# One core, a two-layer decoder trunk: one ring of three PSUM banks in the attention stage, the attention's rows first in the output product, and the convolution's norm moved to the last attention rounds

## The reference, cut to what matters

```python
def conv_sparse_attn_mixer(h, pos, n_keys, w_in, conv_w, conv_b, ln_g, ln_b, w_out):
    a_val, a_gate, q, k, v, qi, ki, wi = jnp.split(h @ w_in, offsets, axis=-1)
    a = a_val * jax.nn.sigmoid(a_gate)
    a = jax.nn.silu(layer_norm(causal_depthwise_conv(a, conv_w, conv_b), ln_g, ln_b))   # 512 channels, width 31
    ...
    o = sparse_index_attention(q, k, v, qi, ki, wi, topk).reshape(bsz, length, ATT_WIDTH)  # 8 heads of 64
    return jnp.concatenate([a, o], axis=-1) @ w_out                                     # (1024, 1024)
```

## Time and profile before

| | us |
|---|---|
| median of 3 runs (lowest, highest) | 2590.16 (2589.67, 2592.37) |
| the profiled execution's own time | 2592.61 |
| its span, first to last instruction | 2590.8 |
| attention stage, first scores to last `normalise` | 391.0 to 623.8 |
| output product of layer 0: first matmul, start of its third block | 630.86, 657.45 |
| PE busy, span | 2412.0 (93%) |
| DVE busy, span | 2029.2 (78%) |
| ACT busy, span | 1684.9 (65%) |

### The profile page before, as it was taken

The page is one execution under the profiler, slowest core; times in us unless marked ns, Lnnn a source line. Parts: engine busy times, 40 slices in busy tenths (PEclk is TensorE's granted clock), DMA queues, the critical chain, the costliest instruction groups (busy, mean ns, idle before and its releaser), DMA issues. The chain is left out here.

```text
span 2590.8 us, 37548 instructions
## 1 busy us (share of the span) xinstructions
PE 2412.0 (93%) x12649; PEld 2071.5 (80%) x12649; DVE 2029.2 (78%) x2588; ACT 1684.9 (65%) x1815; POOL 643.5 (25%) x481
## 2 busy tenths in 40 slices
PE   8989998986979999999999599998979999999997
PEld 8969978874867888888888499996867888888885
DVE  3788876776888999899988543547778998998886
ACT  3369836666227887888887465663147878887775
POOL 0105814353012222222221412121002222222223
PEclk9999999997988999999999699999979999999998
DMA  5502354324339699988898411114259699999994
GB/s 173 141 6 93 82 98 132 100 67 127 108 140 379 228 354 370 363 330 325 310 375 295 179 57 33 41 33 154 96 202 346 237 348 371 374 373 367 376 371 181
DMA packets 121517, 565.80 MB, mean 218 GB/s; under 512 B 23735, under 2 KB 32183, under 8 KB 72144
## 3 DMA queue, kind: packets, MB, share of 16 engines
q1 hardware_dynamic: 96304, 513.25, 54.8%
q0 software_dynamic: 25120, 51.36, 7.2%
HBM read 575.32 MB, written 73.28 MB: 250 GB/s over the span
## 5 line engine op out<-in xcount | busy, mean ns | idle before, releaser
L2197 DVE TENSOR_TENSOR e0wlo<-e0raw,e0whi 128x2048 fp32r<-128x2048 f32 x214 | 487.1, 2290 | 59.9 <-ACT e0whi L2045 59.9
L2045 ACT ACTIVATE e0whi<-e0raw 128x2048 fp32r<-128x2048 f32 x214 | 409.8, 1915 | 92.3 <-PE e0banks L94 78.3
L2197 DVE TENSOR_TENSOR e1wlo<-e1raw,e1whi 128x2048 fp32r<-128x2048 f32 x138 | 313.1, 2286 | 42.4 <-ACT e1whi L2045 42.4
L2045 ACT ACTIVATE e1whi<-e1raw 128x2048 fp32r<-128x2048 f32 x138 | 263.9, 1913 | 42.5 <-PE e1banks L94 36.4
L92 PE MATMUL e0banks<-e0whi,e0xh 128*128 128x512 f32 x576 | 231.1, 401 | 1.1 <-DVE e0xl L2202 1.1
L94 PE MATMUL e0banks<-e0whi,e0xl 128*128 128x512 f32 x576 | 226.4, 393 | 0.0
L93 PE MATMUL e0banks<-e0wlo,e0xh 128*128 128x512 f32 x576 | 225.9, 392 | 0.0
L2197 DVE TENSOR_TENSOR e_wu<-e1raw,e_wu 128x2048 fp32r<-128x2048 f32 x70 | 160.3, 2292 | 17.3 <-ACT e_wu L2045 17.3
L92 PE MATMUL odd_banks<-h2T_hi,odd_w_hi 128*128 128x348 f32 x480 | 171.5, 357 | 0.8 <-DVE h2T_lo L2517 0.5
L2045 ACT ACTIVATE e_wu<-e1raw 128x2048 fp32r<-128x2048 f32 x70 | 134.2, 1918 | 49.0 <-PE e1banks L94 30.1
L93 PE MATMUL odd_banks<-h2T_lo,odd_w_hi 128*128 128x348 f32 x480 | 155.1, 323 | 0.0
(11 more groups left out here) (516 smaller groups left out, 6875.2 us busy)
## 6 DMA issues: line engine op xcount, KB each, us to landing
e0raw<-in_moe_w_gate SPq DMA_DIRECT2D x72, 1024.0 KB
e0raw<-in_moe_w_up SPq DMA_DIRECT2D x72, 1024.0 KB
e0raw<-in_moe_w_down SPq DMA_DIRECT2D x72, 1024.0 KB
e1raw<-in_moe_w_gate SPq DMA_DIRECT2D x70, 1024.0 KB
e1raw<-in_moe_w_up SPq DMA_DIRECT2D x70, 1024.0 KB
e1raw<-in_moe_w_down SPq DMA_DIRECT2D x70, 1024.0 KB
qki_w_raw<-in_w_even SPq DMA_DIRECT2D x22, 512.0 KB, 5.8
pre<-in_conv_band SPq DMA_DIRECT2D x32, 320.0 KB, 3.0
```

The costliest lines, as they stand in the source:

```text
L2045: act.activation(w_hi[i], raw[:, i, :], ACT.Copy).then_inc(hi_done[i], 1)
L2197: dve.tensor_tensor(w_lo[i], raw[:, i, :], w_hi[i].bitcast(F32), ALU.subtract).then_inc(lo_done[i], 1)
```

## The change

- **Banks.** `c_ps` is gone; `t_ps` has three banks, and everything small goes through them as a ring in one fixed order of uses (`ring_order`): transposed groups, convolution groups, denominators, means, variances. Each use waits until the use three places ahead of it has been read (`bank_free`). The scores of blocks 0 to 3 go to the third bank of `s_ps`, those of blocks 4 to 7 to the first two, block 8 to all three; PE waits only for the last step that shares a bank.
- **Convolution.** Groups run in the rounds n with n % 7 not 1, 3 or 5 (four of seven), the last in round 49. ACT takes a group before the late part of `p_high`.
- **Norm.** The means are one burst of 8 groups per tile, in rounds 9, 23, 37 and 51, summed by DVE. POOL, not DVE, centres, behind all its head splits; POOL's split of the output weights comes after that. ACT squares in rounds 57 to 60, variances in 58 to 61, each added by DVE; root in 63, scaling in 65 to 68, tanh in 67 to 70, last product in 69 to 72.
- **Rows through DRAM.** The eight stores stay in the attention's block, but nothing in it waits for them; the wait and the four loads are the first thing that SP does in the output product.
- **Output product of layer 0.** The attention's rows (and their weights) come first. PE makes rows 0 to 3 of block 0, rows 0 to 3 of block 1, then rows 4 to 7 of block 0, then rows 4 to 7 of block 1. ACT and DVE split the inputs of the first two pieces, then weight rows 2 to 7, then the inputs of the last two. Layer 1 keeps its order.

```diff
-GROUP_ROUNDS = [n for n in range(N) if n % 3 != 2][:CG - FIRST_GROUPS]
+GROUP_ROUNDS = [n for n in range(N) if n % 7 not in (1, 3, 5)][:CG - FIRST_GROUPS]
...
-MEAN_AT, CENTRE_AT, VAR_AT, ROOT_AT, SCALE_AT, SWISH_AT, OUT_AT = (CONV_STEPS + n for n in (1, 6, 8, 13, 15, 17, 18))
+MEAN_IN = {GROUP_ROUNDS[W4 * (t + 1) - 1 - FIRST_GROUPS] + 2: t for t in range(CT)}
+CENTRE_AT, VAR_AT, ROOT_AT, SCALE_AT, SWISH_AT, OUT_AT = (CONV_STEPS + n for n in (6, 8, 13, 15, 17, 19))
+T_RING = 3
...
+def ring_order():
+
+    uses = [("conv", g) for g in range(FIRST_GROUPS)]
+    at, norm_at, k = [None] * N, [], 0
+    for n in range(-1, ROUNDS):
+        conv = [("conv", GROUP_IN[n])] if n in GROUP_IN else []
+        turned = []
+        if n + 1 < N:
+            at[n + 1] = k
+            turned = [("turned", k + i) for i in range(len(key_groups(STEPS[n + 1][1])))]
+            k += len(turned)
+        uses += turned[:EARLY_GROUPS] + conv + turned[EARLY_GROUPS:] if late_conv(n) else conv + turned
...
+        def score_banks(b):
+            first, last = (2, 3) if WIDTH[b] <= 512 else (0, -(-WIDTH[b] // 512))
+            return range(first, last)
...
-            sp.wait_ge(stored, 16 * PH)
-            for t in range(CT):
-                sp.dma_start(aT[:, t, :], a_d[P * t:P * (t + 1), :, :].rearrange("c r n -> c (r n)")).then_inc(a_loaded, 16)
             sp.wait_ge(loaded, 64 * HEADS)
-            sp.wait_ge(a_loaded, 16 * CT)
...
             for h in range(1, HEADS):
-                if h == HEADS - 1:
-                    ahead.split_all(pool, out_hi, out_lo)
                 for part in range(4):
                     split(h, part)
+            pool.wait_ge(mean_done, CT)
+            for t in range(CT):
+                pool.tensor_tensor(tile(t), tile(t), every(mean), ALU.subtract).then_inc(cen_done, 1)
+            ahead.split_all(pool, out_hi, out_lo)
...
+            def bank_free(*use):
+                i = nth_use[use] - T_RING
+                kind, k = uses[i] if i >= 0 else ("none", 0)
+                if kind == "turned":
+                    pe.wait_ge(t_free, k + 1)
+                elif kind == "conv":
+                    pe.wait_ge(conv_done, k + 1)
+                elif kind == "mean":
+                    pe.wait_ge(mean_done, k + 1)
+                elif kind == "var":
+                    pe.wait_ge(var_done, k + 1)
+                else:
+                    pe.wait_ge(ready, 1)
...
-                if n:
-                    pe.wait_ge(s_read, n)
+                before = [m for m in range(n) if set(score_banks(STEPS[m][1])) & set(score_banks(b))]
+                if before:
+                    pe.wait_ge(s_read, before[-1] + 1)
...
+    PLAN = [(what, i) for k in range(ahead.split - 1, K)
+            for what, i in [("weights", k)][k < ahead.split:] + [("piece", i) for i, one in enumerate(pieces) if one[3] == k]]
...
         def _(sp):
+            if load_more is not None:
+                load_more(sp)
             for k in range(A, K):
...
-            product(0)
-            pe.wait_ge(p_loaded, 64)
+            for n, k0, k1, _ in pieces[:-1]:
+                run(n, [(k, j) for k in range(k0, k1) for j in range(2)])
+            _, k0, k1, _ = pieces[-1]
+            last_run = [(k, j) for j in range(2) for k in range(k0, k1)]
...
+            def load_conv(sp):
+                sp.wait_ge(conv_stored, 16 * PH)
+                for t in range(CT):
+                    sp.dma_start(aT[:, t, :], a_d[P * t:P * (t + 1), :, :].rearrange("c r n -> c (r n)")).then_inc(a_loaded, 16)
...
-            mix_out(nc, "m0", const, [(aT, CT, True), (oT, 4, False)], A["w_out0"],
-                    A["h0"], A["ln_mix0"], A["wr0"], A["rb0"], h1_d, s1_d, logits, picks, 0, ahead, (4, 4), score[:, 0:4 * D])
+            mix_out(nc, "m0", const, [(oT, 4, False), (aT, CT, True)], A["w_out0"],
+                    A["h0"], A["ln_mix0"], A["wr0"], A["rb0"], h1_d, s1_d, logits, picks, 0, ahead,
+                    [(0, 0, 4, 1), (1, 0, 4, 1), (0, 4, 8, 7), (1, 4, 8, 7)], score[:, 0:4 * D], load_conv, {2: conv_loaded})
```

More of the change, by code:

```diff
@@ L962 @@
 AHEAD, EARLY_GROUPS, DEN_AFTER = 3, 2, 2
[L965 to L977, removed]
+ROUNDS = N + 3 * DEN_AFTER
 def denominator_at(n):
@@ L1223, in _ @@
             turned(0, False)
-            for n in range(N + 3 * DEN_AFTER):
-                three = n + 1 < N and len(key_groups(STEPS[n + 1][1])) > EARLY_GROUPS
+            for n in range(ROUNDS):
                 if n + AHEAD < N:
                     scores(n + AHEAD)
-                if n in GROUP_IN and not three:
+                if n in GROUP_IN and not late_conv(n):
                     taps(GROUP_IN[n])
@@ L1231, in _ @@
                     turned(n + 1, True)
-                if n in GROUP_IN and three:
+                if n in GROUP_IN and late_conv(n):
                     taps(GROUP_IN[n])
@@ L1239, in _ @@
                     denominators(t, g)
-                if MEAN_AT <= n < MEAN_AT + MEAN_STEPS:
-                    means(range((n - MEAN_AT) * CG // MEAN_STEPS, (n + 1 - MEAN_AT) * CG // MEAN_STEPS))
+                if n in MEAN_IN:
+                    means(MEAN_IN[n])
                 if VAR_AT <= n < VAR_AT + CT:
@@ L1638, in split @@
                 ins.then_inc(x_hi_done, 1)
-            split_first(0)
-            for k in range(S, K):
-                act.wait_ge(loaded[k % RAW], 16 * (k // RAW + 1))
-                act.activation(w_hi[k], raw[k % RAW], ACT.Copy).then_inc(w_hi_done, 1)
-                if k - S + 1 < len(first_parts):
-                    split_first(k - S + 1)
-            split(1)
+            for what, k in PLAN:
+                if what == "piece":
+                    split_piece(k)
+                else:
+                    act.wait_ge(loaded[k % RAW], 16 * (k // RAW + 1))
+                    act.activation(w_hi[k], raw[k % RAW], ACT.Copy).then_inc(w_hi_done, 1)
             for n, b in enumerate(blocks):
@@ L1683, in add_bias @@
                 dve.wait_ge(l_done, n + 1)
-            split_first(0)
-            for k in range(S, K):
-                dve.wait_ge(w_hi_done, k - S + 1)
-                dve.tensor_tensor(w_lo[k], raw[k % RAW], w_hi[k].bitcast(F32), ALU.subtract).then_inc(w_lo_done, 1)
-                if k - S + 1 < len(first_parts):
-                    split_first(k - S + 1)
+            for what, k in PLAN:
+                if what == "piece":
+                    split_piece(k)
+                else:
+                    dve.wait_ge(w_hi_done, k - S + 1)
+                    dve.tensor_tensor(w_lo[k], raw[k % RAW], w_hi[k].bitcast(F32), ALU.subtract).then_inc(w_lo_done, 1)
             link(dve.tensor_copy(picks.tri[:].rearrange("p a n -> p (a n)"), const[:, C_TRI:C_TRI + 2 * P]))
-            split(1)
             dve.wait_ge(p_loaded, 64)
@@ L1728, in _, with run @@
         def _(pe):
-            def product(n, beside=None):
+            def run(n, order, beside=None):
                 q = toks(blocks[n])
-                if n:
-                    pe.wait_ge(x_lo_done, n)
-                if n >= 2:
-                    pe.wait_ge(normed, 2 * n - 2)
-                order = [(k, j) for k in range(K) for j in range(2)] if n == 0 else [(k, j) for j in range(2) for k in range(K)]
                 for i, (k, j) in enumerate(order):
-                    if n == 0 and k >= S:
+                    if n < 2 and j == 0:
+                        pe.wait_ge(first_lo, 1 + next(i for i, one in enumerate(pieces) if one[0] == n and one[1] <= k < one[2]))
+                    if n < 2 and k >= S:
                         pe.wait_ge(w_lo_done, k - S + 1)
-                    if n == 0 and j == 0 and k in starts:
-                        pe.wait_ge(first_lo, starts.index(k) + 1)
                     last = mm3(pe, y_ps2[n % 2][0:q, j, :], (x_hi[:, n % 2, k, 0:q], x_lo[:, n % 2, k, 0:q]),
@@ L1746, in product @@
                         beside(i)
+            def product(n, beside=None):
+                pe.wait_ge(x_lo_done, n - 1)
+                pe.wait_ge(normed, 2 * n - 2)
+                run(n, [(k, j) for j in range(2) for k in range(K)], beside)
             def turn(n):
@@ L1785, in beside @@
                             turn(n)
-                product(n + 1, beside)
+                if n == 0:
+                    run(1, last_run, beside)
+                    pe.wait_ge(p_loaded, 64)
+                else:
+                    product(n + 1, beside)
                 if last:
```

168 lines of the change are left out of this document (97 added, 71 removed).

## The result

The changed kernel takes 2610.47 us (median of 4 runs, 2606.71 to 2613.55) against 2591.26 of the one before (4 runs). The medians are 19.2 apart; the ratio is 1.0068 (17.6), 95% interval 1.0056 to 1.0080, so 14.5 to 20.7 slower. The prediction said 2594 and a range to 2603: the time lies outside the range, and slower had 0.43 against 0.42 for no change, which is no call of the side. The profiled execution took 2613.55 (span 2611.8), the longest of the four. Times are microseconds.

What follows compares the result with a forecast made beforehand. PE bounds attention up to round 44, then waits for DVE, table loads and ACT. Attention's gain of 21.0 is outweighed by a late norm and open trip: 660.8 - 657.45 + 0.5 = +3.9, so 2594 against the median; range 2585 to 2603.

Steps and rivals of the forecast that it cites:

- the third block: Output product's third block on PE: forecast to start at 660.8 against 657.45 before.
- the clock: TensorE's clock around the output product's two pauses: +0.5 taken, up to 3 as the bound.
- rounds 0 to 44: Attention's first part: third bank removes most PE waits for low parts; gain 5, between ends of 0 and 8.
- the trip: Stores, loads and weights from the norm's end to the third block's start: little hidden now, +44.8.
- Rounds 45 to 66: Attention's later rounds: 84.1 becomes 68.1, gain 16.0, from DVE's centring and the tanh leaving; ends 10 and 22.
- POOL's centring: Four centrings on POOL against rounds 57 to 60: 9.7 in all, just fits, priced at nothing; bound +4.
- The rival: Rounds 57 to 60: head 7's load or slow POOL centring holds ACT; +4 to +9, 2598 to 2603; chance 0.20.
- The tail: Last rounds, limited by ACT: norm ends 25.7 after step 68's high part, at 616.0; attention near 618.
- The rival without new waits: Last rounds: tanh of tiles 2 and 3 finds its slot free, norm ends 4 to 5 earlier; 2589.5; chance 0.15.
- In the rest PE is the limit and the start is passed on: After the third block's start: its delay of 660.8 against 657.45 carries through to the end unchanged.
- the first rival: Attention up to round 66: PE never starved, gain 8 + 22.7, not 21.0; 2584.5; chance 0.14.
- the parts named for "slower": Verdict slower than 2595.3: rest of the forecast, POOL and the cold clock; given 0.43.

Runs made afterwards that it cites:

- entry_banks: Changed kernel with the first two convolution groups in the output banks, off the ring; ratio to the kernel before 1.0053, 3.9 faster than the changed kernel.
- own_bank: Changed kernel without the shared ring: two banks for transposes and denominators, the third for convolution, means and variances, first three groups not waiting for a memset; ratio 1.0074.
- norm_early: Changed kernel with convolution groups in two of three rounds again, POOL's centrings ahead of its split of head 7; ratio to the kernel before 1.0009.
- weights_first: Changed kernel with SP issuing the weights' rows 4 to 7 ahead of the loads of the convolution's rows; ratio to the kernel before 1.0049.
- product_next_round: Changed kernel with the norm's last product one round behind the tanh, not two; ratio to the kernel before 1.0049, 4.9 faster than the changed kernel.
- mended: Changed kernel with the diffs of entry_banks, product_next_round and tile_stores; ratio to the kernel before 0.9999, 18 faster than the changed kernel.
- tile_stores: Changed kernel with the convolution's rows stored tile by tile behind each product, 32 quarter stores for 8; ratio to the kernel before 1.0027.
- early_mended: Changed kernel with the diffs of norm_early, entry_banks, product_next_round and tile_stores, and the old output product; median 2578.15 us, ratio to the kernel before 0.9943.
- before_tile_stores: Kernel before the change with its stores issued tile by tile behind each product of the norm; ratio to the kernel before 0.9979, 5.4 faster.

## Why the prediction was wrong

It put the third block 3.4 behind (3.9 with the clock); it is 15.45 behind. The step that failed most is the first of the sum, rounds 0 to 44, which was to win 5 and lost 2.9. The entry (3.1) and the backlog behind the third block (2.5) were put at nothing, and the trip was 4.0 short. The mechanism that made it slower, a norm that ends late with its trip open behind it, was forecast. Step by step, with the norm's end 8.1 later than forecast and the way from there 4.0 longer:

- **The stage before**, untouched, ended 2.1 later in this execution. No forecast could have it, and it is no part of the change.
- **The entry was left out: +3.1.** The diff puts the first three groups in the ring and so behind its memset (now first on DVE, with head 0's low parts behind it). The step never looked at where they were before. entry_banks shows it: 3.1 back at the scores.
- **Rounds 0 to 44: -5 forecast, +2.9 measured** (rounds 1 to 44 by the marks). The 5 was a choice between 0 and 8, with no row for it. Two errors. PE's work grew by 2.1 (115.5 busy before, 117.6 after), not 0.2: next to none of the old four bursts of means ended in these rounds, so three came in for none. And waiting, which was to fall by 5, went from 9.7 to 10.5. The ring does win: 3.0 with the new schedule (13.5 of waiting in own_bank), 1.9 with the old one (7.8 in norm_early against 9.7). The schedule of four in seven takes it back: 2.6 with three banks, 3.8 with two. The waits for DVE's low parts are mostly gone, and others stand in their place (waits of PE in these rounds, before and after):

```profile
PE t_ps L1194 <- DVE pT L1347: 5.8, 11, 1.2
PE t_ps L1214 <- DVE pT L1347: 1.9, 2, 1.0
PE c_ps L1157 <- ACT glu L1249: 1.8, 5, 0.4
PE s_ps L1183 <- DVE nmx L1335: 0.6, 2, 0.3
```

```profile
PE t_ps L1230 <- ACT glu L1284: 3.9, 7, 0.8
PE t_ps L1193 <- DVE pT L1379: 1.2, 3, 0.7
PE o_ps L1241 <- DVE oT L1391: 1.1, 1, 1.1
PE s_ps L1219 <- DVE nmx L1367: 1.1, 5, 0.3
PE t_ps L1193 <- ACT glu L1284: 1.0, 2, 0.8
PE t_ps L1250 <- ACT glu L1284: 0.9, 1, 0.9
PE t_ps L1230 <- DVE pT L1379: 0.4, 2, 0.3
PE t_ps L1200 <- DVE pT L1379: 0.2, 1, 0.2
```

  The prediction's own sentence "each use waits for its own kind of the round before, as now" was wrong: a transposed group now waits for a convolution group's take-out, seven times. But that wait comes with the ring, not with the schedule: norm_early has it nine times, 4.2 in all. What four in seven adds to it are the other lines, before the convolution's groups (1.2 against 0.4, and 1.0), the denominators (0.9), the values (1.1) and the scores (1.1 against 0.5). Why they come was not taken apart further.
- **Rounds 45 to 66: -16.0 forecast, -20.3 measured.** The mechanism was right, the size low. The round's rate without a group (2.08) already held waits (2.25 in the five rounds of the earlier trace rows), and the sum added the root, the scaling and 1.5 for the unseen on top, 6.9 in all. Of the 20.3, PE's busy time is 11.5 (65.8 to 54.3), waiting 8.8. Most of the 11.5 goes with the clock: the same score, transpose and value matmuls, each group's time by itself, took 68.9, then 58.3. The clock was granted at 0.95, 0.91 and 0.70 before and at 1.00 after, where PE waited for 9.6 and not for 18.4. In the execution of weights_first, at 0.96 and 0.93, the same program won 18.9 here, so 1.4 of the 20.3 is luck. The Trainium skill (TensorE: Matmul & The Clock Gate, Part 1, "What's actually happening") has the idle array at half rate by default, with activity releasing it; rows and rule agree, here and in the tail, where 0.69 stands beside 9 of waiting in 20.3.
- **POOL's centring: nothing forecast, nothing measured.** 2.23 each, 0.5 of waiting. The rival falls. By the exclusion that the Trainium skill states (SBUF — State Buffer, "Who interferes with whom") POOL's centrings were to meet no such instruction of DVE, and the trace agrees: they take 2.22 to 2.24, all four alike, and DVE has none with two SBUF inputs from 566.0 to 574.8. Where the two do meet, in the last rounds, it is POOL that waits: one of its lines took 1.43 to 1.46 and not 0.45 each time DVE's scaling or product (1.2 to 1.3) fell on it, so eight lines took 3.51 alone and 4.51 beside tile 2's product. That is 1.0 in the chain to the norm's end; the prediction had it in its 4.66.
- **The tail was right.** From step 68's high part (598.8) to the norm's end 25.3, forecast 25.7; waits 2.1 and 2.7, forecast 2.1 and 3.0. The attention's own end, forecast near 618, is 625.6, 1.5 behind the norm's (forecast 2). The rival without new waits falls; product_next_round shows that the two-round distance makes them.
- **The trip: +44.8 forecast to the third block, +48.8 measured.** Stores landed at +16.2 (16.4) and PE started at +13.2 (13.6). The loads of 2.1 MB lay ahead of the weights in the queue, and the first split came at +26.3 (25.1), the last of four at +30.3 (28.9); the convolution's part began at +32.9 (31.6) and PE's matmuls lay 0.43 apart, half rate, until 662, some 2.3 more (0.23 apart behind it). I took the old landing times, 1.24 apart, for a queue that was empty then; here they are 1.25 to 1.43 apart.
- **"In the rest PE is the limit and the start is passed on"** failed. The new order has DVE finish block 0 later: 16.3 from the third to the fourth block, 14.5 before, and 18.0 late at the experts' stage. By the trace the change so costs 18.0 - 2.1 = 15.9, inside the measured interval of 14.5 to 20.7; the other 3 to the end are not tied to the change.
- **Small slips of the working.** The PE part of rounds 45 to 66 adds up to 61.2, not 61.4; the first rival comes to 2584.3, not 2584.5; the parts named for "slower" add up to 0.46, not 0.43; and DVE's 17.39 is not more than the 17.9 that it is held against. None moves the forecast.

With rounds 0 to 66 forecast right, it would still have been short by the entry, the trip and the backlog. The way the parts hang together is simpler than my sum: with eight stores behind the norm, the experts' stage starts 157.8 to 159.9 behind the norm's end in all ten kernels of the table that have them, whichever order the product has; with the stores by tile it is 148 in mended and 149 in tile_stores, and 151 and 154 in early_mended and before_tile_stores, where the norm ends well ahead of the attention. With the eight stores the norm's end was what set the time, and the change moved it by 18.5 to win 2.6 at the last value product (619.5 to 616.9).

## What to carry to other kernels

When a chain with a transfer at its end is moved later in a stage, time the whole chain to its last consumer first; work that leaves the rounds is not gone if it comes back behind them. Store a result in the pieces in which it becomes ready: that alone was worth 11 here and 5 in the kernel before. And give the kernel before the same mend before you judge a mended change: level with the old kernel was 5 slower than the old kernel with its stores mended. Before you read a run as "it doesn't matter", look in the trace at how many places its edit reached. When a buffer joins a shared ring, list its first uses (what they wait for at the stage's start) and, for each use, which other kind now stands a ring's length ahead. When a product is cut so that two blocks finish together, ask when the engine behind it gets the first one.

## What was unexpected of the hardware

The length of SP's issue is not a price per transfer. Eight stores of 260 KB took 12.16, the first two 0.33 and 0.49, the later ones 1.4 to 2.4; of 32 stores of 65 KB the last eight took 0.30 to 0.63, mostly 0.43. The rows are moved at 90 to 214 GB/s in that time, the loads and weights behind them at about 400, so the later large stores were probably held back by the transfers ahead; that was not tried by itself. And a wait in the middle of a product costs twice: 6.5 of standing still, then half rate for some 5 (matmuls 0.43 apart, not 0.23), which is 2.3 more.
